# Gates of a mixer: column products replaced by two units of seven block products

## What is computed

```python
u = rms_norm(h, g_mix)
q_a, k_a, v_a, q_b, k_b, v_b, f_b, gate_logits = split(u @ w_in)
y_a = sliding_window_attention(q_a, k_a, v_a, sinks) @ w_br_swa     # 8 heads, 2 kv heads, window 128
y_b = forgetting_attention(q_b, k_b, v_b, f_b + b_forget) @ w_br_fox  # 8 heads, causal, decayed scores
gates = sigmoid(gate_logits).reshape(B, S, 2, D_MODEL)
h = h + (gates[:, :, 0] * y_a + gates[:, :, 1] * y_b) @ w_mix_out
```

## Time and profile before

| | us |
|---|---|
| median of 3 runs | 1804.68 (1804.1 to 1805.8) |
| profiled execution | 1804.05 |
| its span | 1802.3 |
| TensorE busy | 1758.3 |
| VectorE busy | 1023.3 |
| ScalarE busy | 671.3 |
| GpSimd busy | 265.1 |

### The profile page before, as it was taken

The page is one execution under the profiler, slowest core; times in us unless marked ns, Lnnn a source line. Parts: engine busy times, 40 slices in busy tenths (PEclk is TensorE's granted clock), DMA queues, the critical chain, the costliest instruction groups (busy, mean ns, idle before and its releaser), DMA issues.

```text
span 1802.3 us, 21080 instructions
## 1 busy us (share of the span) xinstructions
PE 1758.3 (98%) x8533; PEld 1479.7 (82%) x8533; DVE 1023.3 (57%) x1377; ACT 671.3 (37%) x1049; POOL 265.1 (15%) x350
## 2 busy tenths in 40 slices
PE   7999999999899999999999999999999999999998
PEld 7888787888899888887888888888887788888886
DVE  5432143432798443489957965984887256445423
ACT  4322244442698431453323322323344244222212
POOL 2000011110687225100000000000002132000101
PEclk9999999999999999999999999999999999999999
DMA  5434524214772445075173247227311112211232
GB/s 177 135 110 137 164 82 132 77 51 118 173 141 48 141 161 201 29 276 187 58 260 136 94 152 268 70 72 287 108 48 36 47 67 103 65 49 46 70 117 93
DMA packets 107600, 215.65 MB, mean 120 GB/s; under 512 B 7984, under 2 KB 28016, under 8 KB 105072
## 3 DMA queue, kind: packets, MB, share of 16 engines
q1 hardware_dynamic: 107504, 214.31, 36.2%
HBM read 170.21 MB, written 44.07 MB: 119 GB/s over the span
## 4 chain that ended last, share of the span: by engine, by line
PE 85%; DVE 6%; DMA 2%; ACT 2%; POOL 2%; issue 1%; SPq 1%; POOLq 0%; ACTq 0%; DVEq 0%
PE PS L649 16%; PE PS L651 16%; PE PS L650 16%; PE PS L883 10%; PE PS L885 10%; PE PS L884 10%; PE PS L625 3%; DVE WB L1705 1%; DMA QS<-qa_scratch 1%; PE PS L753 1%; POOL TF L1990 1%; PE PS L798 1%; DVE PFL L1379 1%; SPq L2084 1%; DMA KO<-kb_scratch 1%
## 5 line engine op out<-in xcount | busy, mean ns | idle before, releaser
L649 PE MATMUL PS<-UH,RHL 128*128 128x512 f32 (+1 forms) x768 | 294.8, 384 | 4.0 <-DVE UL L1379 2.1
L651 PE MATMUL PS<-UH,RHL 128*128 128x512 f32 (+1 forms) x768 | 290.8, 379 | 0.0
L650 PE MATMUL PS<-UL,RHL 128*128 128x512 f32 (+1 forms) x768 | 290.7, 379 | 0.0
L989 ACT ACTIVATE WH<-WB 128x2048 fp32r<-128x2048 f32 x56 | 107.3, 1916 | 295.1 <-PE PS L885 239.7
L1379 DVE TENSOR_TENSOR WB<-WB,WH 128x2048 fp32r<-128x2048 f32 x56 | 128.3, 2290 | 99.7 <-ACT WH L989 99.7
L883 PE MATMUL PS<-WH,AH 128*128 128x512 f32 x448 | 175.0, 391 | 4.0 <-DVE H L1666 2.3
L883 PE MATMUL PS<-AH,WH 128*128 128x512 f32 x448 | 174.6, 390 | 0.0
L885 PE MATMUL PS<-WH,AL 128*128 128x512 f32 x448 | 174.4, 389 | 0.0
L885 PE MATMUL PS<-AH,WB 128*128 128x512 f32 x448 | 174.3, 389 | 0.0
L884 PE MATMUL PS<-WB,AH 128*128 128x512 f32 x448 | 174.3, 389 | 0.0
L884 PE MATMUL PS<-AL,WH 128*128 128x512 f32 x448 | 174.3, 389 | 0.0
(11 more groups left out here) (219 smaller groups left out, 3246.7 us busy)
## 6 DMA issues: line engine op xcount, KB each, us to landing
WB<-in_w_ff SPq DMA_DIRECT2D x32, 1024.0 KB, 9.2
AH<-uf_scratch SPq DMA_DIRECT2D x21, 1024.0 KB, 5.4
AL<-uf_scratch SPq DMA_DIRECT2D x21, 1024.0 KB, 7.5
RAW<-in_w_in SPq DMA_DIRECT2D x32, 512.0 KB, 3.8
H<-in_x SPq DMA_DIRECT2D x16, 512.0 KB, 10.2
gates_scratch<-GST SPq DMA_DIRECT2D x32, 256.0 KB, 2.1
G<-gates_scratch SPq DMA_DIRECT2D x32, 256.0 KB, 3.0
RAW<-in_pool_in_w SPq DMA_DIRECT2D x16, 512.0 KB, 3.5
```

Of the source, the lines that this page charges most:

```text
L649: pe.matmul(o_ap, sh, mh, start=first, stop=False)
L650: pe.matmul(o_ap, sh, ml, start=False, stop=False)
L651: ins = pe.matmul(o_ap, sl, mh, start=False, stop=last)
L989: return act.activation(dst, src, ACT.Copy, **more)
```

## The change

The gates' product (1024 tokens x 1024 by 1024 x 2048) becomes two units, one per branch. A unit is one 1024 x 1024 x 1024 product by the seven-product scheme of Winograd: the weights' blocks A11 to A22 with sums S1 to S4, the tokens' blocks B11 to B22 with sums T1 to T4, each product 512 x 512 x 512. Three products per unit go on in the PSUM banks of the one before (`g_goes_on`), so a unit keeps sums P1, P2, P1+P6, P1+P6+P7, P5, P5+P3 and P4. All seven are stored in `gates_d`; the output's four quarters are each a sum or difference of two of them (`gate_of`). Those are put together in the branch stage: `GX` holds the second one, VectorE adds or subtracts it (`gates_of`), and the sigmoid waits for that.

Token forms: VectorE copies the blocks of u (high + low) into `TU` and makes T1 to T4 there, between the projections; highs and lows follow and all eight forms are stored to DRAM (`ug_d`). Each product from the third on loads its form (2 MB) into one of two places in `UH`/`UL`, so that u itself is overwritten and loaded again for the value projection. Weight blocks (1 MB each) are loaded straight, four per unit; `kb` is projected with the second half of the tokens first, since two of the blocks go where that half of u lies. The windows' timetable is 112 steps instead of 128, one window each 5.65 steps. The value projection does tokens 4 to 7 first; its slabs use other ring slots and are split in products 12 and 13 and after the gates; two splits of branch weights move into the heads' ninth step. The diff, cut:

```diff
-        gates_d, h2_d = scratch("gates", [16, P, D]), scratch("h2", [P, NT, D])
+        gates_d, h2_d = scratch("gates", [2, 7, 4, P, 512]), scratch("h2", [P, NT, D])
+
+        ug_d = {n: scratch(f"ug{n}", [2, P, 2048]) for n in ("B11", "B12", "B21", "B22", "T1", "T2", "T3", "T4")}
...
+            if i >= N1:
+                return 1, (i - N1) % NRING
+            first = S_vb.idx[0]
+            return 0, (i + 1) % NRING if i < first else ((4, 5, 2, 3)[i - first] if i < first + 4 else (i - first + 2) % NRING)
+
+        def before_in_slot(i):
+
+            return max((j for j in range(i) if ring(j) == ring(i)), default=None)
...
-        S_gt = [slab512(w_in, 0, 2312 + 512 * j) for j in range(4)]
...
+        spills += [("qb", j, h) for j0 in (0, 2) for h in range(2) for j in (j0, j0 + 1)]
+        spills += [("kb", j, h) for h in (1, 0) for j in range(4)]
...
-                at_ = 10 + 6.75 * i + 1.5 * (i // NT)
+                at_ = 10 + 5.65 * i + 1.5 * (i // NT)
...
+        g_order = [(0, p) for p in (2, 1, 6, 7, 5, 3, 4)] + [(1, p) for p in (1, 6, 7, 2, 5, 3, 4)]
+        g_steps = range(len(g_order))
+        g_step = {v: n for n, v in enumerate(g_order)}
+        g_goes_on = (6, 7, 3)
+        g_wide = {1: "A11", 2: "A12", 3: "S4", 4: "A22", 5: "S1", 6: "S2", 7: "S3"}
+        g_tokens = {1: "B11", 2: "B21", 3: "B22", 4: "T4", 5: "T1", 6: "T2", 7: "T3"}
+        g_place = [{"A11": "R5", "A12": "R2", "A21": "a", "A22": "b", "S1": "c", "S3": "a", "S2": "d", "S4": "R0"},
+                   {"A11": "R5", "A12": "d", "A21": "R2", "A22": "R3", "S1": "a", "S3": "R2", "S2": "c", "S4": "R0"}]
...
+        u_blocks = {"B11": (0, 0), "B12": (0, 1), "B22": (1, 1), "B21": (1, 0)}
+        TU = at("TU", OH, [P, 4, 4, 512])
+        TUL = at("TUL", OH, [P, 4, 4, 512], F32R)
+        TH = block("TH", OX + 32 * K, F32R)
...
+        gate_of = {(0, 0): (1, 2, ALU.add), (0, 1): (6, 3, ALU.add), (1, 0): (7, 4, ALU.subtract), (1, 1): (7, 5, ALU.add)}
...
+        GX = [at(f"GX{i}", OX + 32 * K + 4096 * i, [P, 2, 512]) for i in range(2)]
@@ tensor
-            for s in range(4):
-                for j in range(4):
-                    bs = [2 * (j % 2), 2 * (j % 2) + 1]
-                    for h in range(2):
-                        take(bs[h], *gate_copied.of(s, j, h))
-                    products([by_columns(S_gt[s], j, h, bs[h], gate_sum, (s, j, h), u_is("mix", 7)) for h in range(2)], range(8),
-                             [S_gt[s]] if j == 3 else (),
-                             {k: (lambda n=8 * (4 * s + j) + k: windows(n)) for k in range(8)})
-            windows(128)
+            for n in g_steps:
+                fresh = g_order[n][1] not in g_goes_on
+                (mh, ml), wl = g_side(n), g_form(n)[1]
+                for s in range(4):
+                    q = slice(P * s, P * s + P)
+                    take(s, *gate_copied.of(n, s))
+                    on.wait_ge(*gw_low.of(n))
+                    if n >= 2:
+                        on.wait_ge(*ug_in[n % 2].of(n, 1))
+                    for k in range(4):
+                        wh = g_high(n)[:, k, q]
+                        pe.matmul(bank(s), wh, mh[:, k, :], start=(k == 0 and fresh), stop=False, skip_group_check=True)
+                        pe.matmul(bank(s), wh, ml[:, k, :], start=False, stop=False, skip_group_check=True)
+                        ins = pe.matmul(bank(s), wl[:, k, q], mh[:, k, :], start=False, stop=(k == 3), skip_group_check=True)
+                        if k == 1:
+                            windows(8 * n + 2 * s)
+                    ins.then_inc(*gate_sum.up(n, s))
+                    windows(8 * n + 2 * s + 1)
+            windows(112)
...
-            for t0 in (0, 4):
+            for t0 in (4, 0):
                 for t in range(t0, t0 + 4):
-                    take(t, *vb_low.of(t))
-                products([by_tokens(S_vb, t, t, vb_sum, (t,), u_is("mix", t)) for t in range(t0, t0 + 4)], range(8),
-                         [S_vb] if t0 else (), {k: (lambda k=k: heads_due(k)) for k in range(8)} if t0 else None)
+                    take((t + 4) % 8, *vb_low.of(t))
+                products([by_tokens(S_vb, t, (t + 4) % 8, vb_sum, (t,), lambda k: u_again[t0 // 4].all())
+                          for t in range(t0, t0 + 4)], range(8),
@@ scalar
+            def turned_high(name):
+                on.wait_ge(*t_sum.of("T4"))
+                if t_order.index(name):
+                    on.wait_ge(*t_out.of(t_order[t_order.index(name) - 1], 1))
+                copy(TH, TU[:, t_place[name], :, :]).then_inc(*t_high.up(name))
+
+            def gate_high(n):
+                u, p = g_order[n]
+                name = g_wide[p]
+                on.wait_ge(*(gw_in[name].of(u) if name[0] == "A" else gw_sum.of(u, name)))
+                on.wait_ge(*(used[S_kb.idx[1 if n == 0 else 3]] if n < 3 else gate_sum.of(n - 2, 3)))
+                copy(g_high(n), g_form(n)[0]).then_inc(*gw_high.up(n))
+
+            turned_high("T2")
+            projected("qb", 0)
+            split_to(S_qb.idx[-1] + 4)
+            turned_high("T3")
+            projected("qb", 1)
             on.wait_ge(*c_turned.of())
             copy(CT[0:64, :], PS[0:64, 1, 0:P], scale=-1.0).then_inc(*c_negated.up())
-            projected("kb", S_kb)
+            turned_high("T1")
+            projected("kb", 0)
+            turned_high("T4")
+            gate_high(0)
...
+            for n in g_steps:
+                if n < 13:
+                    gate_high(n + 1)
+                for s in range(4):
+                    for step in (8 * n + 2 * s, 8 * n + 2 * s + 1):
+                        for v in swa_steps[step]:
                             window(*v)
-                    for h in range(2):
-                        on.wait_ge(*gate_sum.of(s, j, h))
-                        if (s, j) != (0, 0):
-                            on.wait_ge(*gate_out[h].of(*divmod(4 * s + j - 1, 4)))
-                        copy(GST[h][:, :], bank(2 * (j % 2) + h)).then_inc(*gate_copied.up(s, j, h))
-            for v in swa_steps[128]:
+                    on.wait_ge(*gate_sum.of(n, s))
+                    before = g_tiles.index((n, s)) - 2
+                    on.wait_ge(*(gate_out[s % 2].of(*g_tiles[before]) if before >= 0 else t_out.all()))
+                    copy(GST[s % 2][:, :], bank(s)).then_inc(*gate_copied.up(n, s))
+                    if n in (11, 12) and s == 1:
+                        on.wait_ge(*gate_sum.of(9, 3))
+                        split_to(S_vb.idx[n - 11])
+            for v in swa_steps[112]:
                 window(*v)
+            on.wait_ge(*gate_sum.of(13, 3))
+            split_to(S_vb.idx[3])
...
-                    on.wait_ge(*g_in[hf].of(j, 1))
+                    on.wait_ge(*g_summed.of(j, hf))
@@ vector
+            for n, q in u_blocks.items():
+                high, low = u_quarter(*q)
+                dve.tensor_tensor(TU[:, t_place[n], :, :], high.bitcast(F32), low.bitcast(F32), ALU.add).then_inc(*t_sum.up(n))
...
+            t_sums("T1", "B12", "B11")
+            t_sums("T3", "B22", "B12")
...
             split_to(S_ms.idx[0] + 5)
...
+            t_sums("T2", "B22", "T1")
+            t_sums("T4", "T2", "B21")
...
+            turned_low("T1")
+            projected("kb", 0)
+            turned_low("T4")
+            for name in ("S1", "S3", "S2", "S4"):
+                gate_wide_sum(0, name)
+            gate_low(0)
+            projected("kb", 1)
...
+            for n in g_steps:
+                for k in range(8):
+                    if k == 1 and n < 13:
+                        if n == 6:
+                            gate_wide_sum(1, "S4")
+                        gate_low(n + 1)
+                    if n == 4 and k in (3, 5):
+                        gate_wide_sum(1, "S1" if k == 3 else "S3")
+                    if n == 5 and k == 3:
+                        gate_wide_sum(1, "S2")
+                    if n in (11, 12) and k == 4:
+                        split_to(S_vb.idx[n - 11])
...
+            def gates_of(j):
+
+                for hf in range(2):
+                    on.wait_ge(*g_in[hf].of(j, 1, 1))
+                    dve.tensor_tensor(G[hf][:, :, :], G[hf][:, :, :], GX[hf][:, :, :], gate_of[j // 4, hf][2]).then_inc(
+                        *g_summed.up(j, hf))
+
+            gates_of(0)
...
+                if j < 7:
+                    gates_of(j + 1)
@@ sync
+            store_turned("T1")
+            store_block("B21")
+            on.wait_ge(*spill_sum.of("kb", 3, 1))
+            on.wait_ge(*ug_out.all())
+            gate_block(0, "A21")
+            gate_block(0, "A22")
             for v in spills[16:20]:
                 spill(v)
-            fetch_after(S_kb)
+            store_turned("T4")
+            on.wait_ge(*t_out.all())
+            queries(0)
...
+                u, p = g_order[n]
+                for s in range(4):
+                    for step in (8 * n + 2 * s, 8 * n + 2 * s + 1):
```

(32 more changed lines are left out.)

220 lines of the change are left out of this document (140 added, 80 removed).

## The result

The changed kernel takes 1877.2 us (median of 4 runs, 1876.1 to 1878.9) against 1805.2 for the kernel before in the same session: 1.0393 times, 95% interval 1.0381 to 1.0406. I had forecast 1820, with 1832 as the upper end. The direction was right, the size of the loss 4.6 times too small.

What follows compares the result with a forecast made beforehand. TensorE, busy 1758.3 of 1802.3 us, was taken to set the end. Before the gates 5.0, gate stage -13.8, heads 1 and branch stage 23.4 made +15.6 on 1804.05, less 0.6 above: 1820 us, range 1809 to 1832.

Steps and rivals of the forecast that it cites:

- The branch stage: Branches' products: four gate loads and a VectorE sum make an 11.9 us loop against TensorE's 10.9; 23.4 us more.
- The wait before the gates: Projections before the gates: T2 and T4 delay the first V sum, which frees bank 6; 5.0 us more.
- The forms' stores lie beside projections that need no transfer then: 0: Before the gates: storing the token forms costs nothing, as the projections beside them need no transfer; 0 us.
- four wide sums and a low: Start of product 1 in the gate stage, behind this VectorE work: 0.5 us of waiting.
- The gate stage: Gates and windowed attention: 96 fewer matmuls save 21.7 us, new waits sum to 18.6; 216.1 us, 13.8 less.
- Its first part: Gate stage, what is removed: 672 matmuls instead of 768, windows needing 45.3 us; TensorE works 197.5 us.
- the second queries: Gate stage: the second group's head queries, asked for 9.9 us ahead, make TensorE wait 2.7 us.
- product 13: Gate stage: a gate store behind 6 MB of queued loads holds ScalarE; 6.8 us of waiting, and 2.2 for the clock.
- the 3 MB steps: Gate stage: 3 MB queued for loading after four of the products; 1.5 us of waits.
- windows' small steps behind blocks of 2 us: Gate stage: ScalarE and VectorE serve in order, so windows wait behind wide highs and lows; 2.5 us, bounds 0 and 8.
- moved splits: Forget heads' stage: two splits of the branches' weights move into it; 1 us more, bounds 0 and 2.4.
- C: Rival, much slower: blocks on ScalarE and VectorE delay every window, the gate stage gives nothing; 1837 us, chance 0.08.

Runs made afterwards that it cites:

- e2: The kernel after with four staging buffers for gate tiles instead of two, so that ScalarE waits for the store four tiles back: 1860.8 us.
- e1: The kernel after with the second kept sum neither loaded nor added in the branch stage, so the gates are incomplete: 1851.7 us.
- e13: The kernel after with four staging buffers, windows' sum at 13.25 steps, early gate start, reordered branch stage, heads' splits moved later, slabs' splits and loads earlier: 1810.3 us.
- e7: The kernel after with B21's store moved behind the first window group's queries, and A21 and A22 waiting for B22's store alone: 1873.4 us.
- e14: e13 without the early start of the gates, A21 and A22 again loaded behind all blocks' stores: 1813.7 us.
- e15: e13 with the wait for all spills and the bias table's load moved behind the first product's gate stores and the load of T2: 1811.0 us.
- e16: e14 with the bias load moved as in e15: 1813.6 us.
- e12: The kernel after with four staging buffers and the windows' sum at 13.25 steps, nothing else: 1836.8 us.
- e5: The kernel before with its windows every 5.65 steps instead of 6.75, everything else as it was: 1818.8 us, 1.0076 times.
- e6: The kernel after with each window's sum at 13.25 steps after its start instead of 14.5: 1859.1 us.
- e17: The kernel before with windows 5.65 steps apart and each window's sum at 13.25 steps instead of 14.5: 1804.1 us, 0.9984 times.
- e11: The kernel after with the two splits in the first forget heads moved from the 20th and 40th event to the 80th and 120th: 1870.4 us.

## Why the prediction was wrong

**The branch stage (+23.4 forecast, +26.4 measured): right.** Forecast were a first product 13.7 us into the stage (587.6 to 601.3, for which the prediction shows no working), four loads in 5.4 us, a loop of 11.9, and lows 50.6 and 102.9 us in. Measured were 13.2; 6.2 us from the end of half 1's second product (649.90) to its last load's sum (656.15); 12.6; and 53.4 and 108.1. The four loads took a little more than my upper bound of 6.0 there; in e2, whose branch stage is the same code, they took 5.3 (632.54 + 0.68 to 638.54), the loop 11.7, and the stage 104.75, which is 23.1 more than before. So the 5.4 was sound, and 26.4 is the upper end of the scatter. The Trainium skill, DMA: Bandwidth & Descriptors, section Anatomy of one DMA, gives the cost per byte for another path (gpsimd); with the 3.6 us of two loads it made an estimated 4.8, and both traces are above that. e1 shows that nothing but the second kept sum is in this stage's loss, and e13 that another order around it takes nearly all of it away.

**The wait before the gates (5.0 forecast): right.** TensorE waited 3.5 us for the V sum, and the next projection began at 99.94 instead of 94.77, 5.2 later.

**"The forms' stores lie beside projections that need no transfer then: 0": wrong, +7.3, of which 5.5 is the wait for the first form's low.** I looked for transfers that TensorE needed while the stores ran, and found none. What I left out is that SyncE itself waits for the stores, to know that the places are free, before it loads A21 and A22, and that VectorE then has 12 us of sums and a low in front of the first product. The step's own figure, 0.5 for "four wide sums and a low", held for a start of the loads in time; they came 10.6 us late for VectorE. e7, and the pairs e13/e14 and e15/e16, show that moving the stores about brings 3 us at most: the late start, the late form and the late bias change places. The other 1.8 of the 7.3 has no cause of its own in the rows; the clock in the stretch was 0.97.

**The gate stage (-13.8 forecast, +24.7 measured, of which 0.5 was for its start): the step that failed.** Its first part held: 197.5 us of work for TensorE. In e12, 219.94 minus the waits of 5.6, 5.3, 4.6 and 1.0 leaves 203.4, and at the stretch's clock of 0.97 that is an estimated 197 at full clock. Several waits held as well: 2.4 us for the second queries (forecast 2.7), and 5.85 us in product 13 (forecast 6.8; part of the 6.2 for PRL), where ScalarE stood 8.9 us for a gate store behind the 6 MB. The wait for the first reloaded form, 3.6, was more than the 1.5 that I had for all the 3 MB steps. Two terms were missing or mis-sized.
First, I took the new timetable's length (5.6 steps between queries and use) for the queries and did not carry it to bank 7. The distance between a window's sum and the next one's values fell from 2.75 steps to 1.65, and 12 values waited, 20.3 us. e5 shows the same wait without any block product (12.0 us of waits, 13.3 of time), e6 and e17 that the sum's place cures it. My term "2.5 us, windows' small steps behind blocks of 2 us" was the nearest, with a bound of 8: it looked at what stands ahead on ScalarE and VectorE, and not at what the timetable itself had lost.
Second, ScalarE copies a gate tile every two steps now, where it copied two every eight before, and with two buffers each copy holds it to a store two tiles back. I had priced that in product 13 alone. It waited 39.6 us for stores over the stage, seven times, and everything of the windows on ScalarE stood behind; 13.8 of it was for stores that SyncE issued only at 213.33. e2 takes 15.1 us off the stage by buffers alone. Together with the sum it is 34.7, and then the stage is 219.9 against the 216.1 forecast. Whether the two are worth more together than apart (15.1 and 15.5) is open: the stage of the kernel after, 254.6, is the shortest of four of its kind, and against their other three (256.8 to 257.6) the two add up within 2 us.
Of the 254.6 us, 197.5 are the forecast's work and 41.6 waits (the list without the 5.5, with the 1.0 at its end). The other 15.5 I put down to half clock behind those waits, without having measured it by itself: 0.94 over 212.9 us of busy time makes an estimated 12.8 of lost clock. In e12 the same remainder is 219.9 - 197.5 - 16.5 = 5.9.

**Value projection and heads (+1 forecast, +6.7 measured): the "moved splits" were mis-sized.** I gave them a pair of splits on VectorE. They cost 4.7 us (e11), of which 1.5 are waits and 3.2 the clock (0.98 over the stage in the kernel after, 1.00 in e11). ScalarE's wait for the slab (1.70 us) stands just ahead of TensorE's wait of 2.31 for PFL; that it is this pause which lowered the clock is argued from the rows.

**The rest, +2.3,** has no own cause in the rows: it begins at half clock after a wait of 8.55 us. With no wait there it is 1133.0 (e1), as before.

Of the rivals, C (the blocks delay every window and the gate stage gives nothing, 1837) pointed to the right stage with a lower bound of -2; I held its worst case for the end of the range, and the true figure was +24.7. The range lacked a case in which the stage gets longer.

Nothing here beats the kernel before by the change: repaired, it is 0.2% slower (e13). The one kernel with a lower median is e17, the kernel before with two numbers of its timetable changed, 0.16% (0.07 to 0.25), which is less than the 0.2% that the prediction held a measurement of this kernel unable to tell from none.

## What to carry to other kernels

When a change shortens the work under a hand-made timetable, list every pair "last reader of a buffer, next writer" and recompute its distance in the new steps; a distance that still is positive on paper can be too short for the engines in between. A store that nobody on TensorE waits for is not free if the issuing queue waits for it: look for what SyncE does next. And fewer matmuls paid for in transfers need room in the queue in the very stretch where they start; here 96 matmuls (21.7 us) were bought with 65 MB (280.7 moved against 215.7).

## What the runs showed of the hardware beyond that

Waits cost more than their length: in the kernel after, a wait of 5.51 us was followed by starts 0.43 us apart for 4 us, and the waits of the gate stage took its clock to 0.94. Where the waits in the stage fell from 41.6 to 16.5 us (e12), by 25.1, the stage fell by 34.7, and its clock rose to 0.97. A store of 1 MB (half of B21, issued behind other stores and loads) took 17.85 us from issue to landing, where loads of 1 MB one after another had taken 5.4 and 7.5.
